# Three blocks on one core: a pair's four gated sums moved beside its first gated-linear-attention head, and the side work of the last recurrence head cut at whole pieces

## The reference, cut to what matters

```python
def gla_mix(fb, f_up, f_bias, norm_g):
    q, k, v, f_lo, og = _split(fb, (GLA_DK, GLA_DK, GLA_DV, GLA_GATE_LORA, GLA_DV))
    log_alpha = hk(jax.nn.log_sigmoid(f_lo @ f_up + f_bias) / GLA_TAU)      # 4 heads
    def step(s, inp):
        b = jnp.cumsum(la_c, axis=1); b_last = b[:, -1]
        qd = q_c * jnp.exp(b); kd = k_c * jnp.exp(-b)
        att = jnp.where(mask, qd @ kd.T, 0.0)
        o = att @ v_c + qd @ s
        s = jnp.exp(b_last) * s + (k_c * jnp.exp(b_last - b)).T @ v_c
        return s, o
    return head_rms_norm(o, norm_g) * jax.nn.silu(og)
```

## Time and profile before

| | |
|---|---|
| median of 3 runs (lowest, highest) | 4012.46 us (4008.69, 4013.31) |
| the profiled execution, its own time | 4017.6 us |
| span in its profile | 4015.7 us |
| PE busy | 3815.0 us, 95% |
| PE weight loads | 3127.7 us, 78% |
| DVE busy | 1825.7 us, 45% |
| ACT busy | 1355.1 us, 34% |
| POOL busy | 1029.3 us, 26% |
| mean granted TensorE clock | 0.978 |

### The profile page before, as it was taken

One profiled execution on the slowest core, in us unless ns is written; L12 is line 12 of the kernel. 1 busy time (PEld: TensorE's weight loads), 2 busy tenths in 40 slices (PEclk: granted clock), 3 DMA queues, 4 the chain that ended last, 5 costly groups with the idle time before them and its releaser, 6 DMA issues. The chain is left out here.

```text
span 4015.7 us, 44736 instructions
## 1 busy us (share of the span) xinstructions
PE 3815.0 (95%) x18060; PEld 3127.7 (78%) x18060; DVE 1825.7 (45%) x2762; ACT 1355.1 (34%) x2197; POOL 1029.3 (26%) x544
## 2 busy tenths in 40 slices
PE   9999989999999989988899999999998999899998
PEld 7887778887788767877767777888887888687887
DVE  3334653334533365554343645773125362323663
ACT  3223553232322242322332333333323332455332
POOL 0000225551000000001444553554442444332000
PEclk9999999999999999999899999999998999999999
DMA  4232112222223320000112223333331233211332
GB/s 150 95 97 76 49 47 74 83 80 79 85 99 95 96 69 27 22 27 28 58 63 69 81 77 99 96 99 97 97 105 58 95 100 95 59 57 48 95 99 84
DMA packets 90078, 312.42 MB, mean 78 GB/s; under 512 B 10384, under 2 KB 11152, under 8 KB 89616
## 3 DMA queue, kind: packets, MB, share of 16 engines
q1 hardware_dynamic: 89872, 309.56, 24.5%
HBM read 305.29 MB, written 4.19 MB: 77 GB/s over the span
## 5 line engine op out<-in xcount | busy, mean ns | idle before, releaser
L326 POOL TENSOR_TENSOR w_lo<-w_raw,w_hi 128x1024 fp32r<-128x1024 f32 (+1 forms) x353 | 846.1, 2398 | 606.5 <-ACT w_hi L320 589.7
L358 PE MATMUL s_acc<-xn_hi,w_hi 128*128 128x512 f32 x1824 | 718.6, 394 | 42.4 <-DVE xn_lo L1763 16.1
L358 PE MATMUL s_acc<-xn_lo,w_hi 128*128 128x512 f32 x1824 | 713.8, 391 | 0.0
L358 PE MATMUL s_acc<-xn_hi,w_lo 128*128 128x512 f32 x1824 | 713.4, 391 | 0.0
L320 ACT ACTIVATE w_hi<-w_raw 128x1024 fp32r<-128x1024 f32 (+2 forms) x421 | 434.2, 1032 | 608.4 <-PE s_acc L358 505.1
L345 POOL CAST w_hi<-w_raw 128x1024 fp32r<-128x1024 f32 (+1 forms) x167 | 175.7, 1052 | 1610.8 <-issue 961.2
L326 DVE TENSOR_TENSOR w_lo<-w_raw,w_hi 128x1024 fp32r<-128x1024 f32 (+1 forms) x235 | 283.2, 1205 | 362.9 <-ACT w_hi L320 362.1
L358 PEld LDWEIGHTS s_acc<-xn_hi,w_hi 128*128 128x128 f32 x1824 | 344.6, 189 | 123.0 <-DVE xn_lo L1763 17.7
L358 PEld LDWEIGHTS s_acc<-xn_lo,w_hi 128*128 128x128 f32 x1824 | 345.2, 189 | 72.0 <-issue 1.2
L358 PEld LDWEIGHTS s_acc<-xn_hi,w_lo 128*128 128x128 f32 x1824 | 344.7, 189 | 71.9
L358 PE MATMUL s_acc<-hidden_lo,w_hi 128*128 128x512 f32 x784 | 305.3, 389 | 0.0
(11 more groups left out here) (638 smaller groups left out, 6618.8 us busy)
## 6 DMA issues: line engine op xcount, KB each, us to landing
w_raw<-in_f_up SPq DMA_DIRECT2D x132, 512.0 KB, 3.7
w_raw<-in_mg_w SPq DMA_DIRECT2D x64, 512.0 KB, 3.6
w_raw<-in_g_up SPq DMA_DIRECT2D x64, 512.0 KB, 3.6
w_raw<-in_f_down SPq DMA_DIRECT2D x48, 512.0 KB, 3.5
w_raw<-in_hg_w SPq DMA_DIRECT2D x32, 512.0 KB, 3.9
w_raw<-in_g_down SPq DMA_DIRECT2D x32, 512.0 KB, 3.6
w_raw<-in_fox_w SPq DMA_DIRECT2D x24, 512.0 KB, 3.6
w_raw<-in_f_down SPq DMA_DIRECT2D x24, 384.0 KB, 3.1
```

Of the source, the lines that this page charges most:

```text
L326: eng.tensor_tensor(lo, raw, value, ALU.subtract).then_inc(self.parted, 1)
L358: last = pe.matmul(out, w[:, slot, tile_cols(k)], v[:, k0 + k, :], start=start and k == 0 and n == 0, stop=stop and k == kt - 1 and n == 2)
```

## The change

The four sums of a pair go beside its even head; the odd head has none. Thereby heads 0 and 2 have 40 side steps, heads 1 and 3 have 32. `lead` is 4 on even heads and 0 on odd ones. ACT makes four gate sigmoids on even heads and none on odd ones. PE waits, ahead of an odd head's scores, for `gated` of that head in place of `stored` of the one before. In the recurrence head 7 gets stops 16, 8, 8, 0 and 8 (whole pieces) and shares 2, 1, 0 and 2.

```diff
@@ Chunked.tensor
             if leads:
                 steps.wait(pe, "folded", h)
             else:
-                steps.wait(pe, "stored", h - 1)
+                steps.wait(pe, "gated", h)
@@ Chunked.scalar
-            side.scalar(act, self.lead())
+            side.scalar(act, self.lead(h))
@@ Chunked.vector
-            side.vector(dve, q, self.lead())
+            side.vector(dve, q, self.lead(h))
@@ Gla
     def stops(self, h, n):
-        return [8, 8, 8, 4, n - 28] if h % 2 else [20, 4, 4, 0, n - 28]
-
-    def lead(self):
-        return 2
+        return [8, 8, 8, 4, n - 28] if h % 2 else [28, 4, 4, 0, n - 36]
+
+    def lead(self, h):
+        return 0 if h % 2 else 4
 
     def shares(self, h):
-        n = self.beside[h][1] - self.beside[h][0] - 2
+        n = self.beside[h][1] - self.beside[h][0] - self.lead(h)
         return (0, 2, 0, n - 2) if h % 2 else (1, 1, 0, n - 2)
@@ Gla.activate
-        for t in (2 * h, 2 * h + 1):
+        for t in range(2 * h, 2 * h + 4) if h % 2 == 0 else ():
             act.activation(self.unopened[:, t, :], self.unopened[:, t, :], ACT.Sigmoid).then_inc(self.opened, 1)
@@ Hgrn
+    def stops(self, h, n):
+        return super().stops(h, n) if h < self.HEADS - 1 else [16, 8, 8, 0, n - 32]
+
+    def shares(self, h):
+        if h < self.HEADS - 1:
+            return super().shares(h)
+        return 2, 1, 0, self.beside[h][1] - self.beside[h][0] - 3
```

## The result

| | before | changed |
|---|---|---|
| median (lowest, highest) | 4012.45 us (4008.69, 4017.76) | 4020.07 us (4016.43, 4024.40) |
| runs | 14 | 14 |
| ratio, 95% interval | | 1.0018 [1.0011, 1.0025] |
| span of the profiled execution | 4015.7 us | 4022.1 us |

The changed kernel is 7.6 us slower. That is just inside the 0.2% (8 us) that I had called the limit, but its interval excludes no change. The sum had said +4.3, the range 4003 to 4024.

What follows compares the result with a forecast made beforehand. PE, busy 95% of the span, was taken as the bound, movable only through its pauses and the clock after them. 0.7 + 0.4 + 7.2 + 1.5 + 0.5 - 6.0 = +4.3 us on 4012.5, about 4016.5; range 4003 to 4024.

Steps and rivals of the forecast that it cites:

- The odd heads' wait: Heads 1 and 3: PE waits 4.2 us for DVE's output-gate product, held by POOL; net +3.6 us each.
- Heads 0 and 2, kend: Before even heads' scores: the chain starts later too, so no cover is won; +0.7 and +0.4 us.
- the 4 to 6: Sign: in heads 0 and 2 PE's pause for gla_kend is still 4 to 6 us.
- my bound of 1.7: Head 0's kend: with all chain instructions held by POOL, the pause is 6.2 us, +1.7.
- Rival C: POOL holds the chain in heads 0 and 2, and y_lo in odd heads: +8.5 us, 4021; chance 0.20.
- Head 2's bank wait: Head 2's third sum waits 0.85 us for its first sum's bank; +1.5 us (0 to 3).
- half chance of a clock drop: After head 2's bank pause: a half chance of losing 1.4 us to a slower clock.
- The mLSTM's start: The mLSTM's exponentials come 4.9 us earlier, not 5.4: +0.5 us (-1 to +1) on a 4.77 us pause.
- The recurrence's last head: Head 7: the 5.18 us bank pause and its slow clock go, a square wait comes; -6.0 us (-7.5 to -4.5).
- B: Rival: POOL misses the odd heads' product, which then costs +0.8 us; 4007 in all; chance 0.22.
- A: Rival: kend covered in heads 0 and 2, both 4.5 us pauses and their slow clock go; 3998; chance 0.08.
- L2604 took 2.51 us: Sign on DVE's product in odd heads: the forecast is wrong if L2604 takes 0.7 us there.

Runs made afterwards that it cites:

- e4: Changed kernel, but in heads 1 and 3 DVE's output-gate product reads its second input from PSUM, leaving out a factor; 4016.23 us, ratio to before 1.0006.
- e3: Changed kernel, but PE waits for ACT's `activated` instead of DVE's `gated` before odd heads' scores; 4012.16 us, ratio to before 0.9996.
- e9: Changed kernel, but odd heads' `activated` has its own semaphore and PE waits for `stored` as before; 4006.58 us, ratio to before 0.9983.
- e5: Changed kernel, but in even heads DVE takes three sums before the chain and the fourth after `gated`; 4013.15 us, ratio to before 1.0002.
- e1: Kernel before with only the recurrence's half of the change (its stops and shares); 4008.31 us, ratio to before 0.9991.
- e7: Kernel before with the recurrence's half, its stops now 16, 8, 3, 2 and 11; 4006.41 us, ratio to before 0.9989.
- e8: Changed kernel with wait for `activated`, fourth sum late, even stops 28, 4, 3, 1, 4 and recurrence stops 16, 8, 3, 2, 11; 4004.36 us.
- e11: Kernel before with early sigmoids, output-gate semaphore, even stops 20, 4, 3, 1, 4 and recurrence stops 16, 8, 3, 2, 11; 4005.81 us.
- e12: Changed kernel with own output-gate semaphore, fourth sum late, even stops 28, 4, 3, 1, 4, recurrence stops 16, 8, 3, 2, 11; 3995.80 us.
- e2: Changed kernel without the recurrence's stops and shares, so the linear attention's half alone; 4025.35 us, ratio to before 1.0028.
- e10: Kernel before, with odd heads' gate sigmoids made in the even head and an own semaphore for the output gate; 4007.00 us, ratio 0.9982.

## Why the prediction was right, and where it was off

- **The odd heads' wait (+3.6 each).** Right in kind and nearly in size: pauses of 4.20 us twice, +3.0 and +2.9 between scores and updates. The reason given, DVE's product behind POOL's subtraction, is shown by e4 (0.69 us once it reads PSUM). That it is this wait which costs the time is shown by e3 and e9. From 1948 to 1958, the pause and what follows it, the clock was 0.67.
- **Heads 0 and 2, kend.** Right that no cover is won: 6.53 and 3.94 us, both just outside the 4 to 6 that I had named as the sign. The term for head 0 was mis-sized. I took one more instruction held than before, +0.7; all five were, +2.0 (+1.6 to +2.7 over six traces), past my bound of 1.7 in most. Head 2, put at +0.4, came out lower than before (3.94 against 4.37). Rival C was right for head 0 and, as the entry on the mLSTM says, there; in head 2 and in the odd heads, whose y_lo took 0.69 us, it was wrong. e5 shows the tie to the last sum.
- **Head 2's bank wait (+1.5).** The pause is there, 0.59 us for the 0.85 forecast. The half chance of a clock drop was not taken: 1.00 from 1985 to 1990.
- **The mLSTM's start (+0.5).** +1.3: the wait for the exponentials is 6.08 in place of 4.77. My upper bound was 1. ACT now has to wait 1.33 us for y_lo of head 3, which took 2.77 us beside POOL. It took 2.77 before as well, but then it ended before ACT got there.

```profile
2062.40 2.77 DVE L2635 TENSOR_TENSOR y_lo<-gla_g,y_hi 128x512 fp32r<-128x512 f32 x1
```

```profile
2065.25 1.28 ACT L2795 ACT_TABLE_LOAD   x1 [1.33 <-DVE y_lo L2635]
```

- **The recurrence's last head (-6.0).** The step that failed in size: -3.5 in the traces, -4.5 in e1's median. The 5.18 us pause went as said, and the pause for the square came as said (0.69). But I took the stage to end by 932. The row sums came at 925.1, not 923.1. Kend was held (1.41 us, until 905.8), for which I had allowed. But the transposes and first side steps after the scores ran slow, at a clock of 0.66 where it had been 1.00 after the same pause before; I had not charged that, and it is 1.6 us. DVE's output, ending at 933.46, set the end. And the next stage's clock took another 1.6 us. e7, with e8, e11 and e12, shows that earlier row sums end the stage 1.9 us sooner and keep that clock up.
- **The whole.** By the medians the sum was 3.3 us short. In the traces 2.5 of that are the recurrence's half, and the attention's half is 0.6 the other way. The rest I can't place; the spans differ by 6.4, the medians by 7.6. That the attention's sum came so near, 9.7 for 10.3, is in part luck: its parts miss by +1.3, -0.6, -1.4, -0.7 and +0.8 and cancel.
- **The rivals' sums.** Two were added up wrongly. With my own other terms B is 0.7 + 0.4 + 0.8 + 1.5 + 0.5 - 6.0 = -2.1, so 4010.4, not 4007. A's 3998 takes off only its own 14.4 us; with the other terms as forecast (+3.2) it is 4001.3. So B's time lay nearer to the forecast than I wrote. Neither came: L2604 took 2.51 us, against B, and the kend pauses stayed, against A.

## What to carry to other kernels

More work in front of a wait covers nothing when the awaited chain begins only after that same work. A wait that only keeps a counting semaphore in order is not free: give the one event that is out of order its own semaphore. Before a DVE step is put on the path, see in which memory its operands lie and what POOL does just then. Closing one pause shifts the meeting of the two engines, so the gains of single edits can't be taken to add: e8 and e11 fell short of their sums, e12 did not.

## What the runs showed that I had not expected

- In these traces DVE and POOL take turns when both have work on SBUF: five DVE instructions in a row were each held, 1.15 to 2.59 us long, and POOL's casts grew too (1.51 and 1.23 us for 1.05). The Trainium skill, SBUF — State Buffer, section Who interferes with whom, says that the first to issue holds the port for the whole instruction; the traces agree, for the copy from one SBUF tensor (2.50 us) as for products of two. By the same section a product with one SBUF input does not contend with POOL; e4 is such a case, 0.69 us.
- The same pauses don't always bring the clock down. After pauses of 0.69 and 2.09 us the next stage began at a clock of 0.66 in the changed kernel, but at 1.00 in e1, with equal code up to there and the same two pauses:

```profile
932.00:937.00 5.00, 4.83 (x21) 4.03 (x22) 1.23 (x1) 1.06 (x1) 0.00 (x0) 1.00 0.22 73
```

Why it falls in one and not in the other I did not find out, but it is not chance alone. In the seven traces with the change's stops for head 7 and the 2.09 us pause (2.06 in e4), the next stage begins at 0.66 in five and at 1.00 in e1 and e3; in the seven with a pause of 1.03 us it is always 1.00. It is the same behind head 7's scores. With one side step more ahead of them, the way from there to the row sums is 1.6 us longer in nine of eleven traces (19.3 us against 17.65 in e3, 16.5 against 14.83 in e7). The three traces with the old stops, before, e2 and e10, agree within 0.02 us, and the clock there before was 1.00. So each of the two falls takes 1.6 us from the recurrence's half in most executions.
